# Three raw weight buffers instead of four in a two-block transformer kernel

## The chip, the cores and the metric

One core of a Trainium2 chip runs the whole kernel in one launch. The metric is the device time of that launch in microseconds (us), smaller is better; the median of several runs is given.

## The reference

Two transformer blocks over 256 tokens of width 2048, all in float32. The first block is RMSNorm, an input projection, an HGRN2 mixer (gated linear recurrence, 8 heads) beside a forgetting attention (8 heads), an output projection, and a gated FFN of width 5632 with a causal convolution of three taps, then a final RMSNorm. The second block has two layers: a multiscale pool in the first and block attention in the second, each beside a cross-attention to 256 memory tokens, with gates, an output projection and a layer norm. What matters for the change is the shape of each projection:

```python
proj = h @ w_in[l]                       # (256 x 2048) @ (2048 x 7176)
x = x + jnp.concatenate([o_a, o_b], -1) @ w_out[l]
a = h @ w_gate                           # 2048 x 5632, w_up the same, w_down 5632 x 2048
u = h @ w_in[i]                          # second block, 2048 x 4096, twice
y = mixed @ w_out[i]                     # 2048 x 2048, twice
```

All weights, some 360 MB of float32, pass through the core once, for only 256 tokens.

## The kernel before, in words

Every weight matrix is cut into tiles of 128 partitions x 2048 float32 (1 MB; the last tile of each row of `w_ffn_down` is half of that, a tile of `pool_w` is 128 x 1152). There are 348 of them in one list, numbered in the order of use: `add` (L293) appends the tiles of a phase (`in_f`, `in_q`, ... `out1`), so that tiles 0 to 7 are `in_f`, 252 to 255 are the pool's maps, and 256 to 271 are the output projection `out0` of the second block's first layer. A tile goes through four stations:

- **SyncE** transfers it from memory to `raw[:, n % RAWS]` (`sp_phase`, L343, the issue is L355).
- **ACT** writes the higher part, rounded to the matmul's float32r, into `hl_ring[:, n % RINGS, 0]` (`split`, L357, the activation is L366).
- **DVE** writes the rest, raw less higher part, into `hl_ring[:, n % RINGS, 1]` (L369).
- **TensorE** multiplies both parts (`pe_phase`, L459; the matmuls are L451 and L455 in `alternate`, L498 to L500 for the phases of form F, L492 to L494 for the pool's), into one of two pairs of PSUM banks of `G` (the third chunk of `in_f` goes to `SB`).

Semaphores count tiles: `hi_ready` after ACT, `lo_ready` after DVE, `tile_used` after TensorE. SyncE waits on `lo_ready` before it reuses a raw buffer; ACT waits for the transfer and, on `tile_used`, for TensorE to have left tile n - RINGS, with RINGS = 3:

```python
if n >= RAWS:
    eng.wait_ge(lo_ready, n - RAWS + 1)        # SyncE, before tile n
...
if n >= RINGS:
    eng.wait_ge(tile_used, n - RINGS + 1)      # ACT, before tile n
```

`cut_phase` (L420) runs on ACT and DVE: beside tile m of a phase it splits tile m + 2, then does the phase's other work (`between`, evictions, heads, norms), all in program order on that engine. SyncE's program is in order as well, and it does little else than weights.

**The start** is written out by hand. Tiles 0 to 4 come in 18 pieces (`W_PIECES`, L55): tiles 0 and 1 in four pieces of 256 KB each, by turns (pieces 0 to 7), then tiles 2 and 3 in the same way (8 to 15), then tile 4 in two halves (16, 17). Ahead of every second piece SyncE issues a piece of x (`x_given`, L962). The weight pieces are issued at L965 behind the wait of L958; `split_piece` (L380) splits them on ACT (L389) and DVE (L395), and the last piece of a tile is the one that counts in `lo_ready`. TensorE takes the pieces in the same order. Behind tile 5, SyncE issues the constants (`colv`, L967, `fwraw`, L968), then tiles 6 and 7, then x again by rows (`xt`, L971), from which ACT takes the mean square (L1258), and DVE writes `rstd_diag` (L1566) for four small matmuls of TensorE (L1091) behind tile 6.

**Other transfers.** GpSimd issues a few of its own from its software queue, among them a reload of 4 MB of split activations (`bring_back`, L1021 and L1022) once the tensors that it overwrites are free, at `mem_k1` and beside the first tiles of `out0`; there it waits for `pm_l` to reach 4, which DVE gives at L1868 behind the split of tile 258.

The scratch areas are placed by hand (`at`, L118): `raw` begins at 0 KB and has 32 KB, `hl_ring` begins at 32 KB.

Of the kernel before, what the change touches and what calls it, by code (L numbers as in the profile page):

```python
# [48 lines left out]
NEG = -1e30  # L49
SLOT = 2048  # L50
COLS = 318
RAWS = 4
RINGS = 3
X_PIECES = tuple((2 * g, 2 * g + 2) for g in range(8))
W_PIECES = tuple((2 * (g // 4) + c, 2 * (g % 4), 2 * (g % 4) + 2) for g in range(8) for c in range(2)) + ((4, 0, 4), (4, 4, 8))  # L55
# [15 lines left out]
def program(nc, A):  # L71
    ctx = ExitStack()
    with ctx:
# [3 lines left out]
        def sem(name):  # L77
            return ctx.enter_context(nc.semaphore(name))
# [39 lines left out]
        def at(name, kib, shape, dt=F32):  # L118
            return nc.alloc_sbuf_tensor_at(name, shape, dt, offset=base + int(kib * K))

        raw = at("raw", 0, [P, RAWS, SLOT])
        hl_ring = at("hl_ring", 32, [P, RINGS, 2, SLOT], F32R)
# [56 lines left out]

        raw_loaded = [sem(f"raw_loaded{s}") for s in range(RAWS)]  # L180
        hi_ready, lo_ready, tile_used = sem("hi_ready"), sem("lo_ready"), sem("tile_used")
# [158 lines left out]
        def tile_size(p, t):  # L340
            return p.size if isinstance(p.size, int) else p.size[t]

        def sp_phase(eng, name, first=0, end=None):  # L343
            p = phases[name]
            for c in range(p.chunks):
                for t in range(p.tpc):
# [3 lines left out]
                    n = p.tile0 + m  # L350
                    if n >= RAWS:
                        eng.wait_ge(lo_ready, n - RAWS + 1)
                    src = p.source(c, t)
                    dst = raw[:, n % RAWS, 0:tile_size(p, t)].rearrange("p (t n) -> p t n", t=src.shape[1])
                    eng.dma_start(dst, src).then_inc(raw_loaded[n % RAWS], 16)  # L355

# [1681 lines left out]
```

## Time and profile before

| What | Value |
|---|---|
| median of 3 runs | 1995.6 us (1995.56 to 1996.1) |
| the profiled execution, its own time | 1995.86 us |
| its span, first to last instruction | 1994.1 us |
| TensorE busy | 1982.2 us |
| DVE busy | 1249.2 us |
| ACT busy | 873.9 us |
| GpSimd busy | 16.1 us |
| moved by DMA | 391.11 MB, 196 GB/s on the mean |
| granted TensorE clock, mean | 0.998 of full speed |

The span is one profiled execution; its time stands 1.8 us above its span, for what lies around the program. Times in rows are us from the start of the span. In a timeline the bracket at the end is the idle time of the engine just before the instruction, and what ended it. An issue row of SyncE shows how long SyncE needed to issue, not when the data landed; the landing stands in the rows of DMA issues.

### The profile page before, as it was taken

The page shows a single profiled execution, that of the slowest core. Times are in us where ns is not written, and L with a number is a line of the kernel's source. Part 1 is how long each engine was busy: PE and PEld are TensorE (multiplying, and loading weights), DVE is VectorE, ACT ScalarE, POOL GpSimd, SP SyncE. Part 2 cuts the span into 40 slices and gives each one's busy share as a digit, 9 for nine tenths or more (in the row PEclk, how much of TensorE's full clock was granted, in tenths as well). Part 3 has the DMA queues.
Part 4 walks back from the last instruction along what each step waited for, and adds up shares of the span by engine and source line. Part 5 has one row for each costly group of instructions (what it writes and reads, how often), then busy time and mean ns, then how long its engine had stood idle before and what let it go on. Part 6 is the DMA issues. An engine that isn't in the chain of part 4 may idle for free.

```text
span 1994.1 us, 24505 instructions
## 1 busy us (share of the span) xinstructions
PE 1982.2 (99%) x10616; PEld 1701.8 (85%) x10616; DVE 1249.2 (63%) x1149; ACT 873.9 (44%) x833; POOL 16.1 (1%) x53
## 2 busy tenths in 40 slices
PE   9999999999999999999999999999999999999997
PEld 8889888888888888888888888888988888888886
DVE  7766666656666664466666446657866754566665
ACT  7544545454444443344444345343433534344532
POOL 1000000000000000000000000000000000000000
PEclk9999999999999999999999999999999999999999
DMA  9654554776556555655565756745595656644652
GB/s 343 208 171 148 173 173 140 239 264 214 190 179 201 174 196 187 204 189 191 182 198 178 274 181 214 230 158 169 187 337 179 221 190 190 190 148 148 208 194 85
DMA packets 294941, 391.11 MB, mean 196 GB/s; under 512 B 6321, under 2 KB 225201, under 8 KB 293041
## 3 DMA queue, kind: packets, MB, share of 16 engines
q1 hardware_dynamic: 292528, 365.42, 56.3%
q0 software_dynamic: 2304, 24.12, 3.0%
q8 instruction: 84, 1.38, 0.3%
q14 instruction: 25, 0.20, 0.0%
HBM read 381.12 MB, written 8.39 MB: 195 GB/s over the span
## 4 chain that ended last, share of the span: by engine, by line
PE 99%; DVE 0%; DMA 0%; ACT 0%; DVEq 0%; issue 0%
PE G L451 39%; PE G L455 19%; PE G L498 11%; PE G L500 11%; PE G L499 11%; PE SB L795 1%; PE OB L816 1%; PE SB L451 0%; PE G L520 0%; PE G L518 0%; PE G L519 0%; PE OB L819 0%; PE SB L692 0%; PE G L493 0%; PE G L494 0%; PE G L492 0%
## 5 line engine op out<-in xcount | busy, mean ns | idle before, releaser
L369 DVE TENSOR_TENSOR hl_ring<-raw,hl_ring 128x2048 fp32r<-128x2048 f32 (+1 forms) x343 | 772.5, 2254 | 503.1 <-ACT hl_ring L366 502.4
L366 ACT ACTIVATE hl_ring<-raw 128x2048 fp32r<-128x2048 f32 (+1 forms) x343 | 645.6, 1885 | 572.7 <-PE G L500 313.1
L451 PE MATMUL G<-ahl,hl_ring 128*128 128x512 f32 x2080 | 655.2, 396 | 0.2 <-DVE hl_ring L395 0.2
L455 PEld LDWEIGHTS G<-ahl,hl_ring 128*128 128x128 f32 x2080 | 390.9, 188 | 92.3
L455 PE MATMUL G<-ahl,hl_ring 128*128 128x256 f32 x2080 | 408.8, 278 | 0.0
L451 PE MATMUL G<-ops,hl_ring 128*128 128x512 f32 x1216 | 384.3, 397 | 0.0
L451 PEld LDWEIGHTS G<-ahl,hl_ring 128*128 128x128 f32 x2080 | 317.3, 189 | 0.8 <-issue 0.4
L455 PEld LDWEIGHTS G<-ops,hl_ring 128*128 128x128 f32 x1216 | 228.4, 188 | 54.0
L455 PE MATMUL G<-ops,hl_ring 128*128 128x256 f32 x1216 | 239.2, 278 | 0.0
L451 PEld LDWEIGHTS G<-ops,hl_ring 128*128 128x128 f32 x1216 | 185.6, 189 | 0.3
L498 PE MATMUL G<-hl_ring,hhl 128*128 128x512 f32 x352 | 136.9, 389 | 0.0
L499 PE MATMUL G<-hl_ring,hhl 128*128 128x512 f32 x352 | 136.9, 389 | 0.0
L500 PE MATMUL G<-hl_ring,hhl 128*128 128x512 f32 x352 | 136.9, 389 | 0.0
L498 PE MATMUL G<-hl_ring,ops 128*128 128x512 f32 x248 | 96.5, 389 | 0.0
L499 PE MATMUL G<-hl_ring,ops 128*128 128x512 f32 x248 | 96.5, 389 | 0.0
L500 PE MATMUL G<-hl_ring,ops 128*128 128x512 f32 x248 | 96.5, 389 | 0.0
L498 PE MATMUL G<-hl_ring,ahl 128*128 128x512 f32 x224 | 87.6, 391 | 0.0
L500 PE MATMUL G<-hl_ring,ahl 128*128 128x512 f32 x224 | 87.2, 389 | 0.0
L499 PE MATMUL G<-hl_ring,ahl 128*128 128x512 f32 x224 | 87.2, 389 | 0.0
L500 PEld LDWEIGHTS G<-hl_ring,hhl 128*128 128x128 f32 x352 | 66.1, 188 | 13.8
L499 PEld LDWEIGHTS G<-hl_ring,hhl 128*128 128x128 f32 x352 | 66.1, 188 | 13.7
L498 PEld LDWEIGHTS G<-hl_ring,hhl 128*128 128x128 f32 x352 | 66.1, 188 | 13.4
(354 smaller groups left out, 1745.1 us busy)
## 6 DMA issues: line engine op xcount, KB each, us to landing
raw<-in_w_in SPq DMA_DIRECT2D x115, 1024.0 KB, 5.4
raw<-in_w_out SPq DMA_DIRECT2D x48, 1024.0 KB, 5.2
raw<-in_w_ffn_gate SPq DMA_DIRECT2D x44, 1024.0 KB, 5.1
raw<-in_w_ffn_up SPq DMA_DIRECT2D x44, 1024.0 KB, 5.1
raw<-in_w_ffn_down SPq DMA_DIRECT2D x40, 1024.0 KB, 5.2
raw<-in_w_kv_shared SPq DMA_DIRECT2D x24, 1024.0 KB, 5.1
raw<-in_w_mem_kv SPq DMA_DIRECT2D x16, 1024.0 KB, 5.6
ahl<-memop_scratch POOLq DMA_DIRECT2D x2, 4096.0 KB, 14.4
```

The lines of the kernel that those rows point to most:

```text
L366: eng.activation(hi[:, s, 0:size], raw[:, r, 0:size], ACT.Copy).then_inc(hi_ready, 1)
L369: eng.tensor_tensor(lo[:, s, 0:size], raw[:, r, 0:size], hi[:, s, 0:size].bitcast(F32), ALU.subtract).then_inc(lo_ready, 1)
L451: eng.matmul(bank_of(p, c, b), hi[:, s, w], p.rhs(k), start=first and q == 0, stop=False)
L455: last = eng.matmul(bank_of(p, c, b)[:, 0:TOK], lo[:, s, w], p.rhs(k)[:, 0, :], start=False, stop=final and q == len(ks) - 1)
L498: eng.matmul(G[:, bank, :], xhl(k)[:, 0, tok], hi[:, s, w], start=st, stop=False)
L499: eng.matmul(G[:, bank, :], xhl(k)[:, 0, tok], lo[:, s, w], start=False, stop=False)
L500: last = eng.matmul(G[:, bank, :], xhl(k)[:, 1, tok], hi[:, s, w], start=False, stop=sp)
L795: last = eng.matmul(out, l_, r_, start=i == 0, stop=i == len(mm) - 1)
L816: eng.matmul(OB[:, 0:256], H.v(h, 0), pt[:, 0:256], start=True, stop=False)
```

## The change

`RAWS` goes from 4 to 3. It is used in the size of `raw`, in the number of semaphores `raw_loaded`, in the choice of the buffer (`n % RAWS`) and in the waits of SyncE at L352 and L958: the transfer of tile n waits for the split of tile n - 3 where it waited for that of n - 4. Within the first five tiles tile 3 now shares a buffer with tile 0, and tile 4 with tile 1. No offset of another tensor changes.

```diff
--- before.py
+++ after.py
@@ -49,7 +49,7 @@
 NEG = -1e30
 SLOT = 2048
 COLS = 318
-RAWS = 4
+RAWS = 3
 RINGS = 3
 X_PIECES = tuple((2 * g, 2 * g + 2) for g in range(8))
 W_PIECES = tuple((2 * (g // 4) + c, 2 * (g % 4), 2 * (g % 4) + 2) for g in range(8) for c in range(2)) + ((4, 0, 4), (4, 4, 8))
```

## Rows read from the trace of the kernel before

**Rows 1.** The page, part 1: the engines' busy time over the whole span.
```profile
PE 1982.2 (99%) x10616; PEld 1701.8 (85%) x10616; DVE 1249.2 (63%) x1149; ACT 873.9 (44%) x833; POOL 16.1 (1%) x53
```

**Rows 2.** Waits over the span, PE's and SyncE's: us in total, times, longest.
```profile
PE G L451 <- DVE hl_ring L395: 0.2, 1, 0.2
...
SPq L355 <- DVE hl_ring L369: 1785.6, 338, 11.2
```

**Rows 3.** The page, part 6: issues, KB each, median us from issue to landing.
```profile
raw<-in_w_ffn_down SPq DMA_DIRECT2D x40, 1024.0 KB, 5.2
```

**Rows 4.** Timeline of ACT, 1460 to 1477 us: start us, us, [idle before <- releaser].
```profile
1460.46 1.92 ACT L366 ACTIVATE hl_ring<-raw 128x2048 fp32r<-128x2048 f32 x1 [3.52 <-PE G L500]
1465.90 1.92 ACT L366 ACTIVATE hl_ring<-raw 128x2048 fp32r<-128x2048 f32 x1 [3.52 <-PE G L500]
1472.37 1.92 ACT L366 ACTIVATE hl_ring<-raw 128x2048 fp32r<-128x2048 f32 x1 [4.56 <-DMA raw<-in_w_out]
1476.78 1.92 ACT L366 ACTIVATE hl_ring<-raw 128x2048 fp32r<-128x2048 f32 x1 [2.49 <-PE G L500]
```

**Rows 5.** Timeline of SyncE and its DMA issues, 8.31 us: start; KB, us to landing.
```profile
8.31 0.50 SPq L965 DMA_DIRECT2D raw<-in_w_in  x1
...
raw<-in_w_in SPq DMA_DIRECT2D x1, 256.0 KB, 6.5
```

**Rows 6.** DMA issue at 1.24 us, onto empty queues: KB, us to landing.
```profile
raw<-in_w_in SPq DMA_DIRECT2D x1, 256.0 KB, 3.6
```

**Rows 7.** Windows, 14 to 55 us: us, busy of each engine, PEclk, DMA share, GB/s.
```profile
14.00:55.00 41.00, 41.00 (x239) 35.86 (x238) 32.30 (x52) 28.78 (x39) 0.00 (x0) 1.00 1.09 360
```

**Rows 8.** Timeline of DVE, 12 to 43 us: start us, us.
```profile
12.88 1.29 DVE L395 TENSOR_TENSOR hl_ring<-raw,hl_ring 128x512 fp32r<-128x512 f32 x2
...
30.12 2.29 DVE L369 TENSOR_TENSOR hl_ring<-raw,hl_ring 128x2048 fp32r<-128x2048 f32 x1 [0.79 <-ACT hl_ring L366]
...
42.48 0.29 DVE L1566 TENSOR_SCALAR rstd_diag<-ident,nrs 128x128 f32<-128x128 f32 x1
```

**Rows 9.** Timeline of PE, 29 to 46 us: start us, us.
```profile
29.31 0.62 PE L451 MATMUL SB<-ahl,hl_ring 128*128 128x512 f32 x2
...
40.45 0.63 PE L451 MATMUL G<-ahl,hl_ring 128*128 128x512 f32 x2
...
46.03 0.60 PE L1091 MATMUL OB<-rstd_diag,meanw 128*128 128x128 f32 x4
```

**Rows 10.** Timeline of SyncE, 1432 to 1457 us, each issue looked at alone.
```profile
1432.34 0.37 SPq L355 DMA_DIRECT2D raw<-in_w_out  x1
...
1453.50 0.37 SPq L355 DMA_DIRECT2D raw<-in_w_out  x1
...
1456.57 0.37 SPq L355 DMA_DIRECT2D raw<-in_w_out  x1
```

**Rows 11.** DMA issues, 1430.49, 1453.50, 1456.57 us in turn: KB, us to landing.
```profile
raw<-in_w_out SPq DMA_DIRECT2D x1, 1024.0 KB, 5.5
...
raw<-in_w_out SPq DMA_DIRECT2D x1, 1024.0 KB, 6.0
...
raw<-in_w_out SPq DMA_DIRECT2D x1, 1024.0 KB, 15.8
```

**Rows 12.** Timeline of GpSimd (POOL), 1454.64 us.
```profile
1454.64 0.53 POOL L1022 DMA_DIRECT2D ahl<-memop_scratch  x1 [9.27 <-DVE ops L1868]
```

**Rows 13.** DMA queues, 1458 to 1468 us: packets, MB, share of 16 engines.
```profile
q0 software_dynamic: 119, 3.90, 96.3%
q1 hardware_dynamic: 115, 0.23, 6.6%
```

**Rows 14.** Timeline of ACT, 1437 us.
```profile
1437.63 1.92 ACT L366 ACTIVATE hl_ring<-raw 128x2048 fp32r<-128x2048 f32 x1 [0.85 <-PE G L494]
```

**Rows 15.** Timeline of DVE, 1474 us.
```profile
1474.32 2.29 DVE L369 TENSOR_TENSOR hl_ring<-raw,hl_ring 128x2048 fp32r<-128x2048 f32 x1 [3.75 <-ACT hl_ring L366]
```

## The prediction

> **What bounds the kernel now.** I read the page first, then the waits of single engines, then the timelines of the two stretches in which transfers come late. TensorE is busy for 1982.2 of 1994.1 us [rows 1], and the one wait of its own on a split weight tile that the trace shows lasts 0.2 us, at the very start [rows 2]. So a change to how weights are fetched can gain next to nothing; it can only lose, and it loses only where a tile becomes ready after TensorE wants it. SyncE, which issues the weight transfers, waits before 338 of its issues, 1785.6 us in all [rows 2]: it is always early. The question is how much of that earliness the fourth buffer holds up.
>
> Tiles are numbered in the order of use, 0 to 347. A tile is transferred, split by ACT (1.92 us) and by DVE (2.29 us), of which 4.2 us pass from ACT's start to DVE's end [rows 4, 15], and then used. ACT may start on tile n when TensorE has left tile n-3; that is a second ring, of three slots, and it is not changed.
>
> **The change, part by part.** No instruction is added or removed. Every weight transfer n is released by the split of tile n-3 where it was n-4: one tile later.
>
> *Steady state.* TensorE spends 5.44 us on a tile (1465.90 less 1460.46 [rows 4]) and a transfer of 1 MB lands 5.2 us after its issue [rows 3]. Since TensorE never waits for a split tile, the split of n-3 is done at the latest when TensorE starts tile n-3. Then transfer n lands 5.2 us later, and ACT wants it 5.44 us later, when TensorE leaves n-3. So even a split that was finished at the last moment leaves 0.2 us in front of ACT, and behind ACT two tiles of time (10.9 us) stand against a split of 4.2 us, another 6.7 us. A stall needs a transfer of over 5.2 + 0.2 + 6.7 = 12.1 us. A split that is done as early as the ring lets it be (4.2 us into tile n-5) leaves 3 x 5.44 - 4.2 - 5.2 = 6.9 us in front of ACT alone. Cost of the steady state: 0. What hides it is this spare time; where transfers take over 12 us it may be gone. Two stretches come near: the start and the first output projection of the second block.
>
> *The start.* The first five tiles come in pieces. Piece 9 (of 0 to 17, tile 3) was issued at 8.31 us with no wait and landed 6.5 us later, at 14.8 [rows 5]. Now tile 3 shares its buffer with tile 0, and SyncE holds piece 9, and all that is queued behind it on SyncE (x pieces, further weights, the constants, x itself), until DVE has split tile 0's last piece. That is the first of the two of 12.88 us, so about 12.88 + 0.69 = 13.6 [rows 8]. The issue is 5.3 us later. How much later the data is, no row shows. The DMA engines are full until 55 us (360 GB/s, share 1.09 [rows 7]), so what counts is how long they stand idle: what was issued before piece 9 lands by about 14.1 (one piece of 256 KB, 0.7 us at 360 GB/s, before 14.8), and an issue onto empty queues lands in 3.6 us [rows 6] where piece 9 needed 6.5. So it lands at 17.2, 2.4 us later, and everything behind it in the full queue is 2.4 us later. Bounds: 0 if the queue catches up, 5.3 if the whole lateness of the issue goes through. I take 2.4, from the nearest row.
> Who needs it: TensorE takes 5.57 us for a tile here, 1.39 for a quarter, and is done with sixteen pieces at 29.31 [rows 9], so it wants piece 9 at 29.31 - 7 x 1.39 = 19.6; landed at 17.2 and split by 18.6 it is in time by 1.0. The tightest whole tile is 5: split by 30.12 + 2.29 = 32.41 [rows 8], wanted halfway from 29.31 to 40.45, at 34.88 [rows 9]: margin 2.5, of which 2.4 go. The row scale (SyncE, ACT and DVE behind the late x) is written at 42.48 + 0.29 = 42.77 [rows 8] and wanted at 46.03 [rows 9]: margin 3.3, of which 0.9 stays. Cost taken: 0; bounds 0 and 5.3 - 2.5 = 2.8 us.
>
> *The pool stage and tile 256.* Its short tiles use up the spare time. Tile 256's transfer moves from 1430.49 to tile 253's split, the next issue, 1432.34 [rows 10]; with the 5.5 us that it took [rows 11] it lands at 1437.8, and ACT took it at 1437.63 [rows 14]: 0.2 us late for ACT, with some 6 us of other cover before TensorE in a regular stretch, less here. Cost 0.
>
> *The 4 MB reload.* At 1454.64 GpSimd issues a transfer of 4 MB [rows 12]. From 1458 to 1468 us its queue moves 3.90 MB and SyncE's only 0.23 MB [rows 13]: weights stand still for ten microseconds. Before, the transfer of tile 262 was issued at 1453.50 and landed in 6.0 us, at 1459.5; that of 263, issued at 1456.57, was caught and took 15.8, to 1472.4 [rows 10, 11], so that ACT waited 4.56 us for it [rows 4]. Releases stay where they are in time, since the splits of 258 and 259 do; only the tile that each one frees is one earlier. So the issue of 1453.50 now carries 261 and that of 1456.57 carries 262. Tile 261 lands at 1459.5, in time for ACT's 1460.46. Tile 262 lands at 1472.4 where ACT took it at 1465.90: 6.5 us late. Its split then ends where 263's did, 1474.32 + 2.29 = 1476.61 [rows 15], and TensorE leaves tile 261 at about 1476.7 (ACT's row of 1476.78 starts on that [rows 4]). With ACT at 1465.90 it would have been split by 1470.1: a margin of over 6 us shrinks to 0.1. With the semaphore's own time I take a stall of 0.1 us. Bounds: 0, and 3 us if the queue serves it one transfer of 1 MB later (2.9 us at 360 GB/s [rows 7]).
> The rows show 115 packets of the one queue against 119 of the other in these ten microseconds, the bytes 17 to 1 [rows 13]. The Trainium skill (DMA: Bandwidth & Descriptors, Queues, rings and completion order) says that a DMA engine takes turns between queues a packet at a time; the trace agrees, and by that rule any weight transfer still unfinished when the big packets start is held too, which is the first rival. The same page's fit for one DMA, 2.0 us plus bytes at 436 GB/s, would give an estimate of 2.6 us for the piece in place of the measured 3.6; the start would then lose 1.4 us and the sum stays the same.
>
> **Sum.** 0 + 0 + 0 + 0.1 us on the profiled execution's 1994.1 us of span and 1995.86 us of time gives 1995.96. That execution stands 0.26 above the median of the runs, so the forecast is 1995.7 us. Some 0.2% (4 us) is what a measurement of this kernel can tell from no change.
>
> **Rivals.**
> First, slower: tile 261 is caught too. Place: the issue of 1453.50, 1.1 us ahead of the 4 MB. For: it landed at 1459.5, after the 1458 at which the other queue takes over, so it was close. Against: it had that same release and the same neighbours before, and passed. It decides at the point where more than its last packets are left at 1458. Price: landed at 1472.4 it is split by 1476.6, and TensorE wants it at 1476.7 - 5.44 = 1471.2: 5.4 us. Tile 262 then lands 2.9 later and hides behind that. Time 2001.0 us, over the 0.2%.
> Second, the start slides by the whole 5.3 us because SyncE's held issues come too slowly to refill the queue: 2.8 us, 1998.4 us. Against: SyncE issues a piece each 0.5 us [rows 5], the engines need 0.7 for it.
> Third, a shortage at every tile. If transfers took 15.8 us everywhere as the caught one did, three slots would turn in 15.8 + 4.2 = 20.0 us against 16.3, 1.2 us per tile or some 430 us, 2420 us in all. Against: the median is 5.2 [rows 3]. The Trainium skill (Perfetto Trace Analysis, on consistent bubbles) says that a repeated gap on the busy engine can mean too few buffers; no row of TensorE shows any now.
> Fourth, faster, since fewer transfers share the DMA engines: there is only TensorE's wait of 0.2 us to win, 1995.5 us. That the change does nothing at all is excluded by SyncE's 338 waits: each is for the release that moves.
>
> **How the numbers follow.** Forecast (stall under 1 us) 0.80, with the fourth in it 0.01; a part or the whole of the second, or the 3 us bound at tile 262, 0.15; the first 0.04; the third 0.01. Low end 1995.0, the lowest run less the scatter of 0.5 between the runs; high end 1998.4, the second. That leaves out the first and third and what of the middle case adds up. Slower by over 0.2% needs 4 us: 0.05. Faster 0.01. Within 0.2%: 0.94.
>
> **What would show it.** Right: SyncE's first wait stands at piece 9 and ends at 13.6; a dip in DMA rate near 14 to 16 us; the transfers to 55 us some 2.4 us later; TensorE's waits still under 1 us; ACT waiting some 6 us for tile 262's transfer near 1466 to 1472 us, and TensorE idle there 0.1 us or not at all. Wrong: a wait of TensorE of over 1 us near 35 or 46 us (second), or of some 5 us near 1471 (first), or ACT waiting for raw tiles all along (third).

## The result: 2.35 us slower, inside the range but above the point

| | kernel before | three buffers |
|---|---|---|
| median | 1995.68 us (22 runs, 1995.42 to 1996.47) | 1998.03 us (22 runs, 1996.61 to 2003.68) |
| profiled execution, its own time | 1995.86 us | 1997.23 us |
| its span | 1994.1 us | 1995.5 us |

The ratio is 1.0013, 95% interval [1.0008, 1.0019]: a loss of 1.6 to 3.8 us, clear of zero and below the 4 us that the prediction took for the least that a measurement can tell; with this many runs it tells less. The forecast was +0.1 us. New beside the loss is the scatter: the runs of before lie within 1.1 us of each other, those of after within some 7.

The profile after, the page's busy row and chain (to be held against [rows 1]):

```profile
PE 1982.9 (99%) x10616; PEld 1701.9 (85%) x10616; DVE 1249.7 (63%) x1149; ACT 874.4 (44%) x833; POOL 16.0 (1%) x53
...
PE 95%; DMA 2%; DVE 1%; SPq 1%; ACT 0%; issue 0%; DVEq 0%
```

TensorE's work is the same. The chain that ended last was TensorE alone for 99% of the span before; now 5% of it runs through transfers, splits and SyncE's issues.

TensorE's waits in it, all of the span (against [rows 2]):

```profile
PE SB L1070 <- POOL ident L993: 1.7, 1, 1.7
PE G L498 <- DVE hl_ring L369: 0.4, 1, 0.4
PE OB L1091 <- DVE rstd_diag L1566: 0.2, 1, 0.2
```

The first stands before too. The other two are the places that the prediction had called the tightest, and so is a third that is too short for this list: tile 5. Compared tile by tile, by when TensorE releases each, the profiled execution loses 0.20 us at tile 5, 0.42 in and behind L1091 and 0.78 at tile 262, and nothing at any other tile; it began 0.05 us earlier, so it ends 1.34 us later.

*The start.* SyncE's timeline, its longest wait at L965 in the first 60 us, and the window of 14 to 17 us (us, busy of each engine, PEclk, DMA share, GB/s), all after, the window then before as well:

```profile
7.99 6.33 SPq L965 DMA_DIRECT2D raw<-in_w_in  x2
14.36 0.47 SPq L962 DMA_DIRECT2D x_given<-in_x_cols  x1
```

```profile
SPq L965 <- DVE hl_ring L395: 5.4, 1, 5.4
```

```profile
14.00:17.00 3.00, 3.00 (x19) 2.60 (x19) 2.01 (x4) 1.10 (x4) 0.00 (x0) 1.00 0.68 191
```

```profile
14.00:17.00 3.00, 3.00 (x19) 2.60 (x18) 1.65 (x4) 0.76 (x2) 0.00 (x0) 1.00 1.09 362
```

Piece 9 (the second issue of the merged row) waits 5.4 us behind piece 8, to 13.95, 5.6 us later than before, and the DMA rate dips to 191 GB/s. It lands at 16.7, 2.75 us after its issue and 1.9 later than before. The Trainium skill's fit for one DMA (DMA: Bandwidth & Descriptors, Anatomy of one DMA), measured there on GpSimd's transfers, had given an estimate of 2.6 us; the trace agrees with it better than with my 3.6. What follows on DVE and TensorE, after:

```profile
32.56 2.29 DVE L369 TENSOR_TENSOR hl_ring<-raw,hl_ring 128x2048 fp32r<-128x2048 f32 x1 [1.80 <-ACT hl_ring L366]
...
46.08 0.29 DVE L1566 TENSOR_SCALAR rstd_diag<-ident,nrs 128x128 f32<-128x128 f32 x1
```

```profile
46.51 0.68 PE L1091 MATMUL OB<-rstd_diag,meanw 128*128 128x128 f32 x4 [0.16 <-DVE rstd_diag L1566]
```

Tile 5's split is 2.4 us later than in [rows 8], as forecast. It ends at 34.87, 0.14 us before TensorE leaves tile 4, and TensorE loses 0.20 us even so: a split that ends just ahead of the need is not in time. `rstd_diag` is 3.6 us later, not 2.4, and TensorE waits. ACT took the first half of x at 37.26 before and takes it at 39.73 now, 2.5 us later; the second half, which counts, at 39.91 and 43.51, 3.6 us later. Why the second half lands later still is not shown.

*The reload.* SyncE's issue of tile 262, its landing, ACT's row, DVE's row, TensorE's row, after:

```profile
1457.13 0.37 SPq L355 DMA_DIRECT2D raw<-in_w_out  x1
```

```profile
raw<-in_w_out SPq DMA_DIRECT2D x1, 1024.0 KB, 16.2
```

```profile
1473.39 1.92 ACT L366 ACTIVATE hl_ring<-raw 128x2048 fp32r<-128x2048 f32 x1 [10.46 <-DMA raw<-in_w_out]
...
1475.33 2.29 DVE L369 TENSOR_TENSOR hl_ring<-raw,hl_ring 128x2048 fp32r<-128x2048 f32 x1 [6.40 <-ACT hl_ring L366]
...
1477.68 0.50 PE L498 MATMUL G<-hl_ring,ops 128*128 128x512 f32 x1 [0.45 <-DVE hl_ring L369]
```

The transfer that was tile 263's [rows 10, 11] is tile 262's, and takes 16.2 us where it took 15.8. ACT waits 10.46 us, DVE ends at 1477.62, and TensorE, which was out of work at 1477.2, starts at 1477.68.

So the mechanisms that the prediction named at the start and at the reload are there, with their places. The question is the size: why 2.35 us and not 0.1, and what the runs 5 to 8 us above the kernel before are.

### The profile page after: what moved, and what is told of

It is laid out like the page before. It is cut to its first block, busy times and chain, and to the rows that moved or that the text cites. A ratio compares the mean times of both kernels' runs of the same rounds, so it can differ in the third digit from the quotient of the medians.

```text
span 1995.5 us, 24505 instructions
## 1 busy us (share of the span) xinstructions
PE 1982.9 (99%) x10616; PEld 1701.9 (85%) x10616; DVE 1249.7 (63%) x1149; ACT 874.4 (44%) x833; POOL 16.0 (1%) x53
## 4 chain that ended last, share of the span: by engine, by line
PE 95%; DMA 2%; DVE 1%; SPq 1%; ACT 0%; issue 0%; DVEq 0%
PE G L451 38%; PE G L455 19%; PE G L498 11%; PE G L499 11%; PE G L500 11%; PE SB L795 1%; DMA raw<-in_w_out 1%; DMA xt<-in_x 1%; PE OB L816 1%; DVE hl_ring L369 1%; PE G L519 0%; PE G L518 0%; PE G L520 0%; SPq L965 0%; DMA raw<-in_w_in 0%; DMA x_given<-in_x_cols 0%
```

## The experiments

Each was timed against the kernel before on the same chip; us are medians, in brackets the lowest and highest run. "Hold 3" is short for: the transfer waits for the split three tiles ahead; in the kernel before it is four. The first edit is the base of most:

```diff
+def hold(n):
+    return 3
...
-                    if n >= RAWS:
-                        eng.wait_ge(lo_ready, n - RAWS + 1)
+                    if n >= hold(n):
+                        eng.wait_ge(lo_ready, n - hold(n) + 1)
```

and the same at L957. `RAWS` stays 4.

**All transfers held at 3, four buffers in place.**

> Four buffers stay, but every weight transfer waits for the split three tiles ahead, as in the changed kernel. Theory (the cost is the later release alone, not the buffers): as the changed kernel, +1 to +3 us on the kernel before, TensorE waiting some 0.2 us before tile 5, 0.4 us more at L1091 and 0.8 us before tile 262, ACT some 6.5 us late on tile 262. Rival (the addresses or the sharing of the buffers matter): within 0.3 us of the kernel before.

Measured 1998.85 us (1997.83 to 2003.45, 10 runs) against 1995.58, +3.27; ratio 1.0021 [1.0012, 1.0030]. The loss and the scatter are there without a change of buffers or addresses, so the later release is enough for them. The 0.8 us between this kernel's median and the changed kernel's are not told from chance by 10 and 22 runs that scatter by 6 to 7 us. The profiled execution lost 0.45 us at tile 5, 0.40 behind L1091 and 0.47 at tile 262, but also 1.04 us at tile 256, where the prediction had put 0. Its TensorE row:

```profile
1445.25 0.47 PE L498 MATMUL G<-hl_ring,ops 128*128 128x512 f32 x1 [0.78 <-DVE scr L1861]
```

TensorE waits for `scr`, an eviction on DVE, not for a weight tile. That is the third place.

**The start alone.**

```diff
+def hold(n):
+    return 3 if n < 12 else 4
```

> Four buffers; only the transfers of tiles 0 to 11 wait for the split three tiles ahead, all later ones four ahead. Theory (two stalls of the start, small and steady from run to run): +0.4 to +0.8 us, runs within 0.5 us of each other. Rival (the start carries the loss and the scatter of the changed kernel): +2 us or more, with single runs 4 to 8 us up.

1996.44 us (1996.07 to 1997.05, 11 runs) against 1995.58: +0.86, ratio 1.0004 [0.9996, 1.0013]. The interval of the ratio holds 1, but the lowest of these runs is above the highest of the 32 runs of before (1996.01). The start costs some 0.9 us, a little more than the 0.4 to 0.8 expected, and its runs stay within 1 us of each other. Its profiled execution lost 0.13 us at tile 5 and 0.49 behind L1091.

**Everything but the start.**

```diff
+def hold(n):
+    return 4 if n < 12 else 3
```

> Four buffers; the first 12 tiles as in the kernel before, all later transfers wait for the split three tiles ahead. Theory (the 4 MB reload catches tile 262, in some runs 261 as well): +1 to +2 us on the median, single runs up to +8 us. Rival (the start carries it): within 0.3 us of the kernel before.

1997.55 us (1995.53 to 1999.54, 11 runs) against 1995.58: +1.97, ratio 1.0010 [1.0001, 1.0018]. The larger part of the loss, and a spread of 4 us, but no run as bad as expected. The profiled execution was this kernel's luckiest run, 1995.53, and TensorE lost nothing in it: tile 262 was split 0.3 us before its need. The same program loses anything from 0 to 4 us.

**Three buffers, the 4 MB reload late.**

```diff
-RAWS = 4
+RAWS = 3
...
             pool.wait_ge(a_lo, 1)
+            pool.wait_ge(tile_used, phases["out0"].tile0 + 7)
             bring_back(ahl)
```

> The changed kernel with GpSimd's 4 MB reload beside the second block's first output projection held until TensorE has used tile 262. Theory: the stall before tile 262 and the scatter go, the start's stays: +0.4 to +0.8 us on the kernel before, no run above +1.5. Rival (the reload takes any weight transfer that it meets, wherever it stands): +1 us or more again, with a wait of TensorE some 40 us later.

1996.93 us (1996.22 to 1997.96, 11 runs) against 1995.58: +1.35, ratio 1.0008 [0.9999, 1.0017]. With the reload out of the way ACT takes tile 262 on time:

```profile
1466.24 1.92 ACT L366 ACTIVATE hl_ring<-raw 128x2048 fp32r<-128x2048 f32 x1 [2.72 <-PE G L500]
```

The stall there is gone, and no run is above +2.4. But +1.35 was above the +0.4 to +0.8 expected, and five runs are above the +1.5 that was to be the highest. The rival's +1 us came true without its wait: TensorE loses nothing at any tile behind 256. Over a third of the loss is not the start's: this profiled execution lost 0.35 us at tile 256, and 0.45 at tile 5. It lost nothing at L1091; here ACT took the second half of x at 42.16, only 2.3 us later than before.

**The pool's stretch alone.**

```diff
+def hold(n):
+    return 3 if 252 <= n < 258 else 4
```

> Four buffers; only the transfers of tiles 252 to 257 (the pool's maps and the first two of the projection behind them) wait for the split three tiles ahead. Theory (tile 256 lands late for ACT, and on DVE the eviction at L1861, which frees TensorE's next bank pair, is queued behind its split): +0.3 to +1.0 us. Rival (the 4 MB reload is the only late cost): within 0.2 us of the kernel before.

1996.09 us (1995.83 to 1997.18, 11 runs) against 1995.60: +0.49, ratio 1.0002 [0.9993, 1.0011]; all 11 runs are above the median of before. Its ACT and DVE rows at tile 256 (ACT took the tile at 1437.63 before [rows 14]), and the DVE rows of the kernel before:

```profile
1438.49 1.92 ACT L366 ACTIVATE hl_ring<-raw 128x2048 fp32r<-128x2048 f32 x1 [1.73 <-DMA raw<-in_w_out]
```

```profile
1440.44 2.29 DVE L369 TENSOR_TENSOR hl_ring<-raw,hl_ring 128x2048 fp32r<-128x2048 f32 x1 [0.49 <-ACT hl_ring L366]
1442.65 1.26 DVE L1861 SCALAR_TENSOR_TENSOR scr<-G,colv,scr 128x256 f32<-128x256 f32 x3
```

```profile
1439.89 2.29 DVE L369 TENSOR_TENSOR hl_ring<-raw,hl_ring 128x2048 fp32r<-128x2048 f32 x1
1442.09 1.26 DVE L1861 SCALAR_TENSOR_TENSOR scr<-G,colv,scr 128x256 f32<-128x256 f32 x3
```

Tile 256 itself would still be ready 1.3 us before TensorE's 1444.0. But on DVE the eviction at L1861 stands behind its split, and it frees the bank pair into which TensorE writes next: it ended at 1443.35 before and ends at 1443.91 here, 0.56 us later. TensorE's first matmul of the projection, at 1443.85 before, starts at:

```profile
1444.06 0.47 PE L498 MATMUL G<-hl_ring,ops 128*128 128x512 f32 x1
```

Tile 256 is left 0.31 us later than before, so only some 0.25 us of the 0.56 were spare. With all transfers held the eviction came 1.3 us later against TensorE's own progress and cost 1.04, which gives the same margin. The tile's own margin was never the one that counted.

**The reload's stretch alone.**

```diff
+def hold(n):
+    return 3 if 258 <= n < 267 else 4
```

> Four buffers; only the transfers of tiles 258 to 266 wait for the split three tiles ahead. Theory (the reload catches the transfer of tile 262, now and then that of 261): +0.7 to +1.7 us on the median, single runs several us up. Rival (the scatter comes from elsewhere): +0.3 us or less, no run above +1.

1996.02 us (1995.35 to 1997.57, 11 runs) against 1995.60: +0.42, ratio 1.0003 [0.9995, 1.0012]. Below the +0.7 to +1.7 expected, and with more scatter than the rival allowed. Five runs lie 0.3 us around the median of before, one 0.4 above it, and five between +1.3 and +2.0, as if the transfer made it or not. The profiled execution is one of the first five; what the late ones do is open.

**All the regular tiles.**

```diff
+def hold(n):
+    return 3 if 12 <= n < 252 or n >= 267 else 4
```

> Four buffers; all transfers of tiles 12 to 251 and 267 to 347 wait for the split three tiles ahead, those of the start, of the pool and of the reload four ahead. Theory (321 regular tiles cost nothing): within 0.2 us of the kernel before. Rival (a small shortage at many tiles): +0.5 us or more.

1995.55 us (1995.40 to 1996.15, 11 runs) against 1995.60, ratio 1.0001 [0.9992, 1.0009]. 321 tiles cost nothing: the third rival is out. Its profiled execution shows one thing more. The issue of 1453.59, which still carries tile 262 here, stands 1.14 us ahead of the reload's as before, and was caught by it:

```profile
raw<-in_w_out SPq DMA_DIRECT2D x1, 1024.0 KB, 15.6
```

It landed at 1469.2, where the kernel before had it in 6.0 us. With the pool's stretch alone the same issue took 16.9 us. TensorE lost nothing to it, since tile 262 has 6 us to spare with four tiles of hold. That this issue is caught is the event of the first rival.

**Four buffers, the reload late** (the second half of the fourth experiment's edit alone).

> The kernel before (four buffers) with GpSimd's 4 MB reload held until TensorE has used tile 262. Theory (with four buffers nothing waits for the reload, moved or not): within 0.2 us of the kernel before. Rival (moving the reload has a price or a gain of its own, so that the run with three buffers and a late reload can't be read as a cure): beyond 0.3 us either way.

1995.72 us (1995.35 to 1996.04, 11 runs) against 1995.60, ratio 1.0000 [0.9991, 1.0009]. Moving the reload has no price of its own.

**The pool's and the reload's stretch together.**

```diff
+def hold(n):
+    return 3 if 252 <= n < 267 else 4
```

> Four buffers; the transfers of tiles 252 to 266 wait for the split three tiles ahead, the pool's and the reload's stretch together. Alone they gave +0.5 and +0.4 us, all late tiles +2.0. Theory (the lateness of the one stretch is handed on to the other): +1.5 to +2.3 us. Rival (the two add up, and something between regular tiles is missing): +0.7 to +1.1 us.

1997.66 us (1996.82 to 1998.20, 11 runs) against 1995.62: +2.04, ratio 1.0010 [1.0001, 1.0019]. That is all of the +1.97 of the late tiles, and more than twice the 0.49 + 0.42 of the parts: they don't just add. Landings of tile 261's transfer (issued at 1453.1 and 1453.5), first with the reload's stretch alone, then with both, and TensorE's wait with both:

```profile
raw<-in_w_out SPq DMA_DIRECT2D x1, 1024.0 KB, 5.2
```

```profile
raw<-in_w_out SPq DMA_DIRECT2D x1, 1024.0 KB, 7.3
```

```profile
PE G L498 <- DVE hl_ring L369: 1.2, 1, 1.2
```

In these two executions tile 261 lands 2.1 us slower when the pool's stretch is held too, and tile 262 behind it lands at 1473.3 instead of 1471.7. But the one doesn't make the other: with everything but the start held, tile 261's transfer took 8.1 us, and tile 262 landed at 1471.7 all the same, in time. In all five profiled executions in which tile 262's transfer is issued 1.9 us behind the reload (the changed kernel, all held, all but the start, the reload's stretch, both stretches), it lands 2.0 to 2.2 us after the reload itself, and the reload's 4 MB take 15.1 to 16.6 us. So when tile 262 lands is the reload's doing.

A part of what the pool's stretch adds can be read. GpSimd issues the reload when DVE gives `pm_l` behind the split of tile 258, and DVE is late from tile 256 on. In each of the four profiled executions in which DVE is late there (all held, all but the start, the pool's stretch, both), the reload's issue stands 21.78 us ahead of TensorE's end of tile 261; in the kernel before, the changed kernel and the reload's stretch alone 22.06 us. That takes 0.3 us from the margin at tile 262, which was 0.3 us with the reload's stretch alone. The rest of the 1.1 us above the sum of the parts stays open; that the two together cost 2.0 us is shown.

**Three buffers, two 1 MB loads moved behind the reload.** They are issued ten us ahead of the reload and hold the weights' queue as well; I took them for the reason of the worst runs.

```diff
-            for v, row in enumerate(("ln_g", "ln_b")):
-                pool.dma_start(rowbuf[:, v, :], A[row][0:1, :].broadcast_to([P, D])).then_inc(row_loaded, 16)
             pool.wait_ge(pm_l, 4)
             pool.wait_ge(a_lo, 1)
             bring_back(ahl)
+            for v, row in enumerate(("ln_g", "ln_b")):
+                pool.dma_start(rowbuf[:, v, :], A[row][0:1, :].broadcast_to([P, D])).then_inc(row_loaded, 16)
```

> The changed kernel with GpSimd's two 1 MB loads at L1051 issued behind its 4 MB reload instead of ten us ahead of it; the reload stays. Theory (these loads hold tile 260's transfer, so that 261's runs into the reload; that makes the runs of +6 to +8 us): highest run under +3.5 us, median +1.4 to +2.2. Rival (the reload alone catches 261 in the bad runs): median and highest run as the changed kernel, +2.4 and +5 or more.

2005.67 us (2003.98 to 2006.12, 5 runs) against 1995.62: +10.05, ratio 1.0048 [1.0036, 1.0061]. Both expectations fail, for a plain reason that I had missed: the 2 MB now stand right behind the 4, and block the weights for 6 MB on end. It is a dose of the suspected cause instead of a cure. Tile 261 lands in 5.2 us as hoped, but tile 262's transfer takes 21.0 us, and TensorE waits:

```profile
raw<-in_w_out SPq DMA_DIRECT2D x1, 1024.0 KB, 21.0
```

```profile
PE G L498 <- DVE hl_ring L369: 5.4, 1, 5.4
```

From tile 261 to 262 TensorE falls back by 7.7 us, 2.3 more than it waits. The windows of that stretch show where they are (PE busy is the first busy number, PEclk the number ahead of the last two), and the matmuls behind the wait:

```profile
1470.00:1478.00 8.00, 8.00 (x37) 6.45 (x35) 0.00 (x0) 0.00 (x0) 0.00 (x0) 1.00 0.99 401
1478.20:1483.50 5.30, 0.00 (x0) 0.00 (x0) 2.26 (x1) 3.39 (x2) 0.00 (x0) 0.77 0.92 337
1483.60:1491.40 7.80, 7.80 (x25) 6.32 (x26) 4.58 (x2) 2.24 (x2) 0.00 (x0) 0.72 0.86 307
1491.40:1497.00 5.60, 5.60 (x26) 4.65 (x25) 2.46 (x2) 2.03 (x2) 0.00 (x0) 1.00 0.42 144
```

```profile
1483.59 0.80 PE L498 MATMUL G<-hl_ring,ops 128*128 128x512 f32 x1 [5.39 <-DVE hl_ring L369]
1484.18 0.63 PE L499 MATMUL G<-hl_ring,ops 128*128 128x512 f32 x1
...
1487.98 0.39 PE L499 MATMUL G<-hl_ring,ops 128*128 128x512 f32 x1
```

After 5.4 us without work the granted clock is at its lower level, half of full speed (1.2 GHz of 2.4), and the second to the tenth matmul start 0.43 us apart instead of 0.23. The Trainium skill (TensorE: Matmul & The Clock Gate, Part 1) gives 1.2 GHz for the cold array and 2.4 for the warm one; the trace agrees. The stall's price is its length and 2.3 us on top. The profiled execution took 9.2 us more than the one of before; the 1.5 us that are not tile 262's are the start's.

**Three buffers with another order of pieces at the start, and the late reload.** The pieces of tile 2 go all ahead of those of tile 3, with the x pieces 4 to 7.

```diff
-W_PIECES = tuple((2 * (g // 4) + c, 2 * (g % 4), 2 * (g % 4) + 2) for g in range(8) for c in range(2)) + ((4, 0, 4), (4, 4, 8))
+W_PIECES = tuple((c, 2 * g, 2 * g + 2) for g in range(4) for c in range(2)) + tuple((2 + c, 2 * g, 2 * g + 2) for c in range(2) for g in range(4)) + ((4, 0, 4), (4, 4, 8))
+X_AT = {0: 0, 2: 1, 4: 2, 6: 3, 8: 4, 9: 5, 10: 6, 11: 7}
...
-                if i % 2 == 0 and i // 2 < len(X_PIECES):
+                if i in X_AT:
```

> Three buffers, the reload late, and the pieces of tile 2 all ahead of those of tile 3 at the start (x pieces with them), so that SyncE has eight issues to make before it must wait for tile 0's split. Theory (the start's loss is the idle time of the DMA engines behind piece 8): +0.3 to +0.7 us, TensorE not waiting at tile 5 nor at L1091; DMA rate without a dip at 14 to 16 us. Rival (the start's loss is something else about the later release, such as tile 5 or x itself being released late): +1.0 to +1.5 us, as with the late reload alone.

1995.92 us (1995.61 to 1996.82, 11 runs) against 1995.62: +0.30, ratio 1.0002 [0.9993, 1.0010]. Window as above:

```profile
14.00:17.00 3.00, 3.00 (x20) 2.65 (x19) 3.00 (x7) 3.00 (x7) 0.00 (x0) 1.00 1.07 364
```

No dip, and no wait at tile 5 or L1091. Of the 1.35 us with the late reload alone 1.05 are gone, somewhat more than the start's 0.86. What is left is the pool's stretch (0.40 us at tile 256 in its profiled execution). So three buffers can be had for 0.3 us; none of these kernels beats the one before, whose TensorE had next to nothing to win.

**Two tiles ahead, regular tiles only.**

```diff
+def hold(n):
+    return 2 if 12 <= n < 252 or n >= 267 else 4
```

> Four buffers; the transfers of tiles 12 to 251 and 267 to 347 wait for the split TWO tiles ahead, those of the start, pool and reload four. Theory (a regular tile has 6.9 us before ACT and 6.7 behind it, a further tile of 5.4 still fits): within 0.8 us of the kernel before. Rival (the slack was nearly used up by three): +5 us or more, ACT and TensorE waiting for transfers at many tiles.

2009.90 us (2008.85 to 2011.18, 5 runs) against 1995.62: +14.3, ratio 1.0072 [1.0058, 1.0086]. The time is the rival's, the pattern is neither's. TensorE loses nothing from 20 to 1115 us, in over 180 tiles, though ACT waits for transfers at some 30 of them. The loss is in a few places, above all 6.8 us at tile 249, inside the pool's averages. ACT (first) and DVE (second) ahead of it:

```profile
1404.49 1.92 ACT L366 ACTIVATE hl_ring<-raw 128x2048 fp32r<-128x2048 f32 x1 [5.37 <-DMA raw<-in_w_in]
1414.53 0.85 ACT L1425 ACTIVATE pooledhl<-ringscr 128x768 fp32r<-128x768 f32 x1 [8.13 <-DVE ringscr L1848]
...
1415.80 3.69 ACT L366 ACTIVATE hl_ring<-raw 128x2048 fp32r<-128x2048 f32 x2
```

```profile
1406.43 2.29 DVE L369 TENSOR_TENSOR hl_ring<-raw,hl_ring 128x2048 fp32r<-128x2048 f32 x1 [3.86 <-ACT hl_ring L366]
1408.64 0.95 DVE L1838 COPY ringscr<-scr 128x768 f32<-128x768 f32 x1
...
1413.54 0.96 DVE L1848 TENSOR_TENSOR ringscr<-ringscr,scr 128x768 f32<-128x768 f32 x1
```

Tile 248 lands 5.4 us late for ACT, which tile 248 itself can bear: it is split at 1408.7 and wanted at 1410.3. But behind its split DVE has 5.9 us of pool work, behind that ACT has L1425, and behind that stands the split of tile 249. TensorE waits 4.3 us for it, and the clock falls here as well, to 0.50 (window as above):

```profile
PE G L451 <- DVE hl_ring L369: 4.3, 1, 4.3
```

```profile
1418.40:1425.00 6.60, 4.86 (x14) 4.09 (x15) 5.02 (x3) 1.73 (x2) 0.00 (x0) 0.50 0.58 174
```

## Why the prediction came out right in kind and low in size

The range 1995.0 to 1998.4 holds the median of 1998.03, and "within 0.2%" holds. The point was 2.3 us low. That the range holds the median is in part luck: its high end was the price of the second rival, which did not happen; the time got there by the start, tile 256 and the reload together, and the prediction said that it left out what of its middle case adds up. By its steps:

- **Steady state, 0.** Right: -0.05 us for 321 tiles. But the reason given, 12.1 us for any transfer, was too generous. By that sum a hold of two tiles would still have been free, and it cost 14.3 us: work that stands on ACT and DVE behind the split takes its part of the 6.7 us behind ACT.
- **The start, 0 (bounds 0 to 2.8).** Mechanism right: piece 9 held until 13.95 us, tile 5 split 2.4 us later. Size wrong: it costs 0.86 us. Two terms failed. The row scale I moved by the same 2.4 us as the rest; it came 3.6 us later and ate its margin of 3.3 (0.40 to 0.49 us in four profiled executions, nothing in the one in which it came 2.3 later). Tile 5 I left with a margin of 0.1 us and a cost of 0; the profiled executions with the start held and the pieces in their old order lost 0.13 to 0.56 us there.
- **Tile 256, 0.** Wrong, and by a step left out, not by a number: I held the transfer against TensorE's need of that tile and did not ask what else is queued behind its split on DVE. It is L1861, with some 0.25 us of margin. 0.49 us alone.
- **The reload, 0.1 (bounds 0 to 3).** Mechanism right to the issue: the transfer of 1456.57 became tile 262's. Size wrong. Alone it costs 0.42 us, beside the pool's stretch the two cost 2.04, of which 1.55 are above the pool's own. The failed term is the margin of 0.1 us at tile 262, taken as a stall of 0.1. In the five profiled executions in which tile 262 is the tile held behind the reload, its transfer takes between 15.2 and 16.7 us. Every late one is paid and no early one is given back, so the expected cost of such a margin is some of the scatter, not 0. And a split has to end some 0.35 us ahead of the need to cost nothing: where it ended 0.33, 0.28, 0.14 us before TensorE had left the tile ahead, and 0.07, 0.39, 1.13 us after, TensorE lost 0.02, 0.09, 0.20, 0.47, 0.78 and 1.52 us.
- **Sum.** Parts measured alone: 0.86 + 2.04 = 2.9 us, between the +2.35 of the changed kernel and the +3.27 of its twin with four buffers.
- **First rival (tile 261 caught, 2001.0, chance 0.04).** Five of the 32 runs of those two kernels lie at 2001.05 to 2003.68. The rival's price lacked what the experiment with the two loads behind the reload shows, the clock after a stall of 5 us: 5.4 + 2.3 = 7.7 us would give 2003.3. That is near the worst four. Its event is shown: two profiled executions with four tiles of hold there caught that issue, at 1469.2 and 1470.95. Had it carried tile 261, wanted at 1471.3 and 1471.5 and split 4.3 us after landing, TensorE would by estimate have waited some 2 to 4 us, and the clock may have fallen on top, as it did after 4.3 us. But no profiled execution of the changed kernel is one of those runs, so what happens in them stays open. In the late tiles alone or with the pool's and reload's stretches alone no such run came in 22; at five in 32 that can still be chance.
- **Second rival (the start slides by 5.3 us).** Out: of the 5.6 us by which the issue is later, 1.9 reach piece 9's data and 2.4 tile 5's split.

## What to carry to other kernels

A buffer of a prefetch ring is paid for where transfers stand still, not in the steady state: look for the long transfer of another queue and for the hand-made start, and number the release that each issue waits for, since one buffer fewer moves each tile into the place of the next. A margin that one profile shows as 0.1 to 0.6 us is not a cost of 0: here the hand-over took some 0.35 us of it, and the scatter of the landing the rest. And ask for each late transfer not only when its tile is wanted but what is queued behind its split on the splitting engines; at tile 256 the margin that counted was some 0.25 us and not 1.8.

## What the runs showed of the hardware

- One queue with large packets (3.90 MB in 119 [rows 13]) all but stops another with small ones (0.23 MB in 115) for as long as it has work: 4 MB made a 1 MB transfer issued 1.9 us behind them take 15.2 to 16.7 us, 6 MB made it 21.0, against 5.2. Twice it caught one that was issued 1.1 us ahead of it. The Trainium skill (DMA: Bandwidth & Descriptors, Queues, rings and completion order) has the engines take turns by packets; the dose agrees.
- An issue onto drained queues landed in 2.75 us (256 KB), faster than the 3.6 of the program's second issue on which the prediction rested.
- A split that ends less than some 0.35 us before TensorE's end of the tile ahead already delays TensorE: with the split 0.33 us before to 1.13 us after it, TensorE lost 0.02 to 1.52 us.
- Stalls of TensorE of 1.2 and 1.9 us (both stretches held; two tiles ahead) left the granted clock at 1.00. With one of 4.3 us (two tiles ahead, tile 249) it was 0.50 from 1418.4, still within the stall, to 1425 us; one of 5.4 us took it to the lower level for some 6.8 us (a mean of 0.77 over 5.3 us and 0.72 over 7.8) and cost 2.3 us beyond its length.
